# The pooling branch's mixing products taken by token half instead of by group

## The chip, the cores and the metric

The kernel runs on one core of one Trainium2 chip. The metric is device time in microseconds (us), the median of several runs. TensorE (PE) multiplies matrices, and its results can lie only in PSUM, which has eight banks of 128 partitions x 512 fp32 numbers. VectorE (DVE) and ScalarE (ACT) read PSUM, GpSimd (POOL) works in SBUF, and SyncE (SP) queues most of the transfers. Each engine takes its own instructions in the order in which they are written; semaphores hold one engine back for another.

## What is computed

One layer of a hybrid decoder on 1024 tokens of width 1024. The part that the change touches stands in the first block, where a pooling branch and an attention branch run side by side on the same input:

```python
h = rmsnorm(x, norm_mix_g)
u_pool, q, k, v, f_logit, g_logit = jnp.split(h @ w_in, IN_SPLITS, axis=-1)
# pooling: 4 groups of 128 channels, trailing-window mean minus the token
d = ...                                            # (tokens, 4 groups, 128)
y = jnp.einsum('bsgc,gcd->bsgd', d, pool_w)        # the mixing products
y_pool = (y.reshape(B, S, 512) * pool_scale) @ w_pool_out
y_fox = forgetting_attention(q, k, v, f_logit + b_forget) @ w_fox_out   # 8 heads of 64
x = x + (sigmoid(g_pool) * y_pool + sigmoid(g_fox) * y_fox) @ w_out
```

Cross-attention to 256 memory tokens, a SwiGLU feed-forward part and a last RMSNorm follow.

## The kernel before

**Units.** The attention runs as 32 units, u = 8 x (pair of heads) + i, where i is the block of 128 queries. In unit u PE computes the scores of u (L2562, called S here: 6 matmuls up to i = 3, 12 from i = 4), sometimes the products with the values of older units (L2530, V), and the transposes of unit u - 1 (L2539, T). DVE adds the forget bias and finds the largest score (L1915, two instructions), ACT takes the exponential (L1326) and DVE divides by the sum (L1927, L1929, called the norm of u here). The transposes in unit u + 1 wait for the norm of u. S of i < 4 writes banks 0 and 2, S of i >= 4 writes banks 0 to 3; T has banks 4 and 5, V has bank 6.

**Parts and fillers.** Other work of PE is put into the units as fillers, so that PE has something to do while DVE and ACT work on the scores. A unit has two parts, 2u and 2u + 1. For i >= 1 the order on PE is S(u), V, the first two groups of T (all of T, where i <= 4), part 2u, the rest of T, part 2u + 1; for i = 0 it is S, part 2u, V, first two groups of T, part 2u + 1, the rest of T. The tables `FIRST_FILL` (parts 0 to 23) and `NEXT_FILL` (parts 24 to 63) say how many fillers each part takes, in a fixed sequence of 88: 16 pieces of four products left over from the stage before, then 8 mixing products M0 to M7 (L2500, one group and one half of the tokens each), then 64 chunks of the products with `w_pool_out` (L2330 to L2332).

**The chunks.** The output of the pooling branch is made in 16 tiles, v = 0 to 15 (128 output channels c = v // 2, token half h = v % 2). Tile v takes four chunks, written v.0 to v.3 here, one for each group k, of three matmuls each. All 16 tiles are summed in PSUM bank 7. Chunk v.0 therefore waits until DVE has read tile v - 1 out of the bank: `pe.wait_ge(za_done, v)`. That read, `pool_gated(v)` (L1891, called za of v here), multiplies by the gate that SP has loaded into `g_st`. It needs chunk v.3, and its place among DVE's instructions is fixed by the part in which v.3 stands, through the table `GATED_IN`: for an even part it comes right behind the bias of u if i = 0 or i >= 4 and behind the norm of u if i is 1 to 3; for an odd part it comes behind the norm of u.

**The mixing products.** M m writes one bank of `MIX_BANK`; ACT takes the rounded high part `d_hi` (L1333, table `MIXED_IN`), DVE the rest `d_lo` (L1900, tables `LOWS_IN`, at the end of a unit, and `LOWS_LATE`, behind its bias). Before, m counts group by group (g = m // 2, h = m % 2), the banks 3, 7 and 1 go in turn, and tile 0 waits for all eight `d_lo`. Unit 12 is the first after unit 7 whose scores use banks 1 and 3, and its S waits for the first seven `d_lo`.

## Time and profile before

| what | value |
|---|---|
| median of 3 runs (1431.56 to 1432.39) | 1431.56 us |
| the profiled execution | 1431.69 us |
| its span, first to last instruction | 1429.6 us |
| PE busy | 1408.6 us, 99% |
| DVE busy | 992.0 us, 69% |
| ACT busy | 630.3 us, 44% |
| POOL busy | 551.4 us, 39% |
| mean granted TensorE clock | 0.998 |

The span and the 2.1 us around it make up the execution's own time. PE is busy nearly all the time, so the time is what PE has to do plus what it waits. Busy times of PE run over each other: a matmul of 128x512 is shown with some 0.39 us and the next one starts 0.23 us later. Costs are therefore read from one start to the next.

### The profile page before, as it was taken

What the parts mean: (1) busy time and instruction counts of PE and PEld (TensorE: products, weight loads), DVE (VectorE), ACT (ScalarE), POOL (GpSimd) and SP (SyncE); (2) the same over time, 40 slices, a digit from 0 to 9 for tenths busy, and PEclk for the clock granted to TensorE, in tenths of its full rate; (3) what the DMA queues carried; (4) which work ended last, traced back from release to release, by engine and by line L of the source; (5) the groups of instructions that cost most, each with busy time, mean ns of one, the idle gap of its engine ahead of it and who ended that gap; (6) DMA issues with size and microseconds to landing.
All of it is one profiled execution on the core that took longest, in us unless ns stands there. A gap on an engine that the chain in (4) does not pass through costs nothing.

```text
span 1429.6 us, 19604 instructions
## 1 busy us (share of the span) xinstructions
PE 1408.6 (99%) x7122; PEld 1154.2 (81%) x7122; DVE 992.0 (69%) x1442; ACT 630.3 (44%) x1196; POOL 551.4 (39%) x571
## 2 busy tenths in 40 slices
PE   8999999999999999999999999999999999999998
PEld 5878888887677788888888788888888888888886
DVE  7846495546866737877657877776776767785867
ACT  6545343335866644556444532233322332444445
POOL 5833243334545312013013654454444443354402
PEclk9999999999999999999999999999999999999999
DMA  8264264445332298214103112333332335883334
GB/s 215 50 130 117 56 136 101 74 82 202 116 97 84 65 294 215 80 60 133 60 0 147 66 58 93 110 111 111 110 110 84 109 111 204 303 283 100 89 104 148
DMA packets 107145, 172.14 MB, mean 120 GB/s; under 512 B 7293, under 2 KB 63121, under 8 KB 105514
## 3 DMA queue, kind: packets, MB, share of 16 engines
q1 hardware_dynamic: 98016, 146.59, 34.5%
q0 software_dynamic: 5408, 15.76, 4.3%
q10 hardware_dynamic: 3626, 8.54, 1.6%
q8 instruction: 58, 0.95, 0.3%
q14 instruction: 37, 0.30, 0.1%
HBM read 125.42 MB, written 42.30 MB: 117 GB/s over the span
## 4 chain that ended last, share of the span: by engine, by line
PE 88%; POOL 3%; ACT 2%; DMA 2%; DVE 2%; issue 1%; SPq 1%; DVEq 0%; ACTq 0%; POOLq 0%
PE ps L2330 27%; PE ps L2332 27%; PE ps L2331 27%; PE ps L2539 2%; PE ps L2530 2%; PE ps L2562 1%; POOL w_lo L873 1%; DMA w_raw<-in_w_xkv 1%; DMA e_raw<-in_w_in 1%; ACT prob L1326 1%; SPq L669 1%; PE ps L2392 1%; PE ps L2700 0%; ACT w_hi L1135 0%; POOL tok_f L922 0%
## 5 line engine op out<-in xcount | busy, mean ns | idle before, releaser
L2330 PE MATMUL ps<-t_lo,s_hi 128*128 128x512 f32 x308 | 119.9, 389 | 0.1
L2331 PE MATMUL ps<-t_hi,s_hi 128*128 128x512 f32 x308 | 119.8, 389 | 0.0
L2332 PE MATMUL ps<-t_hi,s_lo 128*128 128x512 f32 x308 | 119.8, 389 | 0.0
L2330 PE MATMUL ps<-h_lo_T,w_hi 128*128 128x512 f32 x256 | 100.5, 393 | 1.3 <-ACT u_t L1237 1.0
L1620 DVE TENSOR_TENSOR s_lo<-w_raw,s_hi 128x512 fp32r<-128x512 f32 x77 | 62.0, 805 | 56.3 <-ACT s_hi L1535 56.1
L1535 ACT ACTIVATE s_hi<-w_raw 128x512 fp32r<-128x512 f32 x77 | 48.7, 632 | 118.0 <-PE ps L2332 91.9
L2332 PE MATMUL ps<-h_hi_T,w_lo 128*128 128x512 f32 x256 | 99.7, 389 | 0.0
L2331 PE MATMUL ps<-h_hi_T,w_hi 128*128 128x512 f32 x256 | 99.6, 389 | 0.0
L1551 ACT ACTIVATE p_sb<-ps 128x512 f32<-128x512 f32 x22 | 13.1, 599 | 187.4 <-PE ps L2332 187.4
L2330 PE MATMUL ps<-hf_lo_T,w_hi 128*128 128x512 f32 x212 | 82.5, 389 | 0.0
L2331 PE MATMUL ps<-hf_hi_T,w_hi 128*128 128x512 f32 x212 | 82.5, 389 | 0.0
L2332 PE MATMUL ps<-hf_hi_T,w_lo 128*128 128x512 f32 x212 | 82.5, 389 | 0.0
L1620 DVE TENSOR_TENSOR w_lo<-s_sum,w_hi 128x512 fp32r<-128x512 f32 x64 | 49.3, 774 | 41.8 <-ACT w_hi L1186 41.5
L2330 PE MATMUL ps<-h_lo_B,w_hi 128*128 128x512 f32 x192 | 76.2, 397 | 0.9 <-DVE h_lo_B L1620 0.9
L1038 POOL TENSOR_TENSOR w_sum<-w_raw 128x512 f32<-128x512 f32 x11 | 14.2, 1292 | 158.7 <-DVE w_lo L1620 96.7
L2332 PE MATMUL ps<-h_hi_B,w_lo 128*128 128x512 f32 x192 | 74.9, 390 | 0.0
L2331 PE MATMUL ps<-h_hi_B,w_hi 128*128 128x512 f32 x192 | 74.8, 389 | 0.0
L2330 PEld LDWEIGHTS ps<-t_lo,s_hi 128*128 128x128 f32 x308 | 57.8, 188 | 12.6 <-issue 0.5
L2190 DVE TENSOR_TENSOR hq<-ps,p_sb 128x512 f32<-128x512 f32 x11 | 7.6, 690 | 86.9 <-DMA hs_dram<-h_sum 75.1
L2332 PEld LDWEIGHTS ps<-t_hi,s_lo 128*128 128x128 f32 x308 | 57.8, 188 | 12.0
L2331 PEld LDWEIGHTS ps<-t_hi,s_hi 128*128 128x128 f32 x308 | 57.8, 188 | 11.9
L862 POOL TENSOR_SCALAR ms<-ss 128x1 f32<-128x1 f32 x30 | 11.2, 374 | 141.6 <-ACT junk_x L1141 47.6
(402 smaller groups left out, 4319.0 us busy)
## 6 DMA issues: line engine op xcount, KB each, us to landing
w_raw<-hs_dram SPq DMA_DIRECT2D x77, 256.0 KB, 2.7
raw_p<-in_w_ffn_in SPq DMA_DIRECT2D x22, 512.0 KB, 4.5
w_raw<-in_w_ffn_in SPq DMA_DIRECT2D x22, 512.0 KB, 4.3
hs_dram<-h_sum SPq DMA_DIRECT2D x11, 1024.0 KB, 9.1
hs_dram<-hq SPq DMA_DIRECT2D x11, 768.0 KB, 7.1
wq_B<-in_w_ffn_out SPq DMA_DIRECT2D x8, 1024.0 KB, 7.8
raw_f<-in_w_in SPq DMA_DIRECT2D x14, 512.0 KB, 7.0
gate_dram<-c_st SPq DMA_DIRECT2D x28, 256.0 KB, 2.0
```

What stands on the lines that cost most here:

```text
L669: sp.dma_start(x_t[t][:], x2[tile_of(t), :]).then_inc(x_loaded[t], 16)
L873: nc.gpsimd.tensor_tensor(w_lo[n % SLOTS][:], w_raw[n % RAWS][:], w_hi[n % SLOTS][:].bitcast(FP32), ALU.subtract).then_inc(lo_ready, 1)
L1326: nc.scalar.activation(prob[u % 2][:, a, 0:n], prob[u % 2][:, a, 0:n], ACT.Exp, bias=neg_max[:, u % 2, a:a + 1], scale=-1.0, accum_out=pro ...
L1535: nc.scalar.activation(s2_hi[n % SLOTS2][:], s_raw(n % SLOTS2), ACT.Copy).then_inc(s_split_hi, 1)
L1620: nc.vector.tensor_tensor(out, a, hi.bitcast(FP32), ALU.subtract).then_inc(done, 1)
L2330: nc.tensor.matmul(dst, w_h, x_l, start=start, stop=False, skip_group_check=onto)
L2331: nc.tensor.matmul(dst, w_h, x_h, start=False, stop=False, skip_group_check=onto)
L2332: return nc.tensor.matmul(dst, w_l, x_h, start=False, stop=stop, skip_group_check=onto)
L2392: last = nc.tensor.matmul(ps[0:F_ROWS + HEADS, 5 * h, :], f_w[:, KD * h + 4 * part + j, :], (h_lo if x else h_hi)[ops[part]][:, j, :], sta ...
L2530: last = nc.tensor.matmul(ps[a * DH:(a + 1) * DH, 6, tile_of(v % 2)], v_sb[:, j, hc:hc + DH], turned(v, a)[:, tile_of(j)], start=j == 0, s ...
L2539: last = nc.tensor.transpose(ps[:, 4 + g % 2, tile_of(j - j0)], prob[v % 2][:, a, tile_of(j)], ident[:])
L2562: last = nc.tensor.matmul(ps[:, 2 * a + c // 4, 0:n * P], q[p % 2][head, tile_of(i)], k[p % 2][head, keys], start=term == 0, stop=term == 2)
```

## The change

The mixing products count half by half: h = m // 4, g = m % 4. With the first four `d_lo` (and the fifth, whose product uses bank 7) the even tiles of the first token half can be made, so tile 0 waits for five `d_lo` in place of eight and tile 1 for all eight. `MIX_BANK` becomes a list of eight, `MIX_FREED` says which `d_lo` each product waits for, and the tables for ACT and DVE are renumbered. S of unit 12 now waits for eight `d_lo`.

Tile 0 begins in part 21 (unit 10) in place of part 25 (unit 12). The two fill tables put one more M into part 17, one more into part 20, two chunks into part 21 and one each into parts 22 and 23; parts 29, 37, 41 and 57 each lose one chunk. No matmul, read or transfer is added or taken away.

```diff
-FIRST_FILL = (2, 2, 2, 2, 1, 0, 1, 1, 1, 0, 1, 0, 1, 0, 1, 1, 1, 1, 2, 1, 1, 1, 1, 0)
-NEXT_FILL = ((0, 2, 1, 1, 2, 2, 1, 2) + (1, 2, 1, 1, 2, 2, 2, 2, 2, 2, 1, 1, 1, 1, 1, 2)
-             + (1, 4, 2, 2, 2, 2, 2, 2, 2, 2, 1, 1, 1, 1, 1, 3))
+FIRST_FILL = (2, 2, 2, 2, 1, 0, 1, 1, 1, 0, 1, 0, 1, 0, 1, 1, 1, 2, 2, 1, 2, 2, 1, 1)
+NEXT_FILL = ((0, 2, 1, 1, 2, 1, 1, 2) + (1, 2, 1, 1, 2, 1, 2, 2, 2, 1, 1, 1, 1, 1, 1, 2)
+             + (1, 4, 2, 2, 2, 2, 2, 2, 2, 1, 1, 1, 1, 1, 1, 3))
 DEFER_DONE = {0: 0, 1: 1, 4: 2, 7: 3}
-MIXED_IN = {8: (0, 1), 9: (2, 3), 10: (4, 5, 6), 11: (7,)}
+MIXED_IN = {8: (0, 1, 2), 9: (3, 4, 5), 10: (6, 7)}
...
-GATED_IN = {part: v for part in range(24, 8 * T) for v in range(16) if FILL[part] <= 24 + 4 * v + 3 < FILL[part + 1]}
+GATED_IN = {part: v for part in range(20, 8 * T) for v in range(16) if FILL[part] <= 24 + 4 * v + 3 < FILL[part + 1]}
...
-LOWS_IN = {8: (0, 1), 9: (2, 3), 10: (4,), 11: (7,)}
-LOWS_LATE = {11: (5, 6)}
-MIX_BANK = (3, 7, 1)
+LOWS_IN = {8: (0, 1), 9: (3, 4), 10: (6,)}
+LOWS_LATE = {9: (2,), 10: (5,), 11: (7,)}
+MIX_BANK = (3, 7, 1, 3, 7, 1, 3, 1)
+MIX_FREED = {3: 1, 4: 2, 5: 3, 6: 4, 7: 6}
...
-                    g, h = divmod(m, 2)
+                    h, g = divmod(m, NG)
...
-                    elif m >= 3:
-                        pe.wait_ge(mix_lo, m - 2)
+                    elif m in MIX_FREED:
+                        pe.wait_ge(mix_lo, MIX_FREED[m])
...
                         if v == 0:
-                            pe.wait_ge(mix_lo, 2 * NG)
+                            pe.wait_ge(mix_lo, NG + 1)
                         else:
                             pe.wait_ge(za_done, v)
+                        if v == 1:
+                            pe.wait_ge(mix_lo, 2 * NG)
...
                     if u == 12:
-                        pe.wait_ge(mix_lo, 7)
+                        pe.wait_ge(mix_lo, 2 * NG)
```

Worked out from the tables, the last chunk of a tile and the first of the next (v.3 | v+1.0) stand in these parts:

| tiles | before | after |
|---|---|---|
| 0, 1 | 27, 28 | 23, 25 |
| 1, 2 | 29, 30 | 27, 28 |
| 2, 3 | 32, 33 | 30, 31 |
| 3, 4 | 35, 36 | 33, 33 |
| 4, 5 | 37, 38 | 36, 36 |
| 5, 6 | 39, 40 | 38, 39 |
| 6, 7 | 41, 42 | 40, 41 |
| 7, 8 | 45, 46 | 44, 45 |
| 8, 9 | 48, 49 | 47, 48 |
| 9, 10 | 49, 50 | 49, 49 |
| 10, 11 | 51, 52 | 51, 51 |
| 11, 12 | 53, 54 | 53, 53 |
| 12, 13 | 55, 56 | 55, 55 |
| 13, 14 | 57, 58 | 57, 58 |
| 14, 15 | 61, 62 | 61, 62 |

PE in units 10 to 12 of the kernel before: mixing products (out of `d_in_sb` and `pw_sb`), the scores of unit 11, its transposes, the last mixing product, the scores of unit 12.

```order
L2500 MATMUL ps<-d_in_sb,pw_sb 128x512 [waits mix_lo,d_in1,d_in0] x2
L2562 MATMUL ps<-k_hi1,q_lo1 128x512 [waits sc_biased,qk_lo]
L2562 MATMUL ps<-k_hi1,q_lo1 128x512
L2562 MATMUL ps<-k_hi1,q_hi1 128x512 x2
L2562 MATMUL ps<-k_lo1,q_hi1 128x512 x2
L2539 MATMUL ps<-ident,prob0 128x128 [waits pt_copied,prob_ready]
L2539 MATMUL ps<-ident,prob0 128x128 x2
L2539 MATMUL ps<-ident,prob0 128x128 [waits pt_copied]
L2539 MATMUL ps<-ident,prob0 128x128 x2
L2500 MATMUL ps<-d_in_sb,pw_sb 128x512 [waits mix_lo,d_in1,d_in0]
L2562 MATMUL ps<-k_hi1,q_lo1 128x512 [waits sc_biased,mix_lo,qk_lo]
```

The same place after: the last two mixing products, at once the two first chunks of tile 0 (`w_hi0` is the first piece of `w_pool_out`), then the scores of unit 11.

```order
L2501 MATMUL ps<-d_in_sb,pw_sb 128x512 [waits mix_lo,d_in1,d_in0] x2
L2331 MATMUL ps<-d_lo,w_hi0 128x512 [waits mix_lo,lo_ready]
L2332 MATMUL ps<-d_hi,w_hi0 128x512
L2333 MATMUL ps<-d_hi,w_lo0 128x512
L2331 MATMUL ps<-d_lo,w_hi0 128x512
L2332 MATMUL ps<-d_hi,w_hi0 128x512
L2333 MATMUL ps<-d_hi,w_lo0 128x512
L2565 MATMUL ps<-k_hi1,q_lo1 128x512 [waits sc_biased,qk_lo]
L2565 MATMUL ps<-k_hi1,q_lo1 128x512
L2565 MATMUL ps<-k_hi1,q_hi1 128x512 x2
L2565 MATMUL ps<-k_lo1,q_hi1 128x512 x2
L2542 MATMUL ps<-ident,prob0 128x128 [waits pt_copied,prob_ready]
```

The chunks moved ahead of the scores, and tile 0 waits for part of the `d_lo` alone.

PE in unit 16, part 33, before: the transposes of unit 15, then chunks 3.0 and 3.1, then the rest of the transposes.

```order
L2539 MATMUL ps<-ident,prob1 128x128 [waits pt_copied]
L2539 MATMUL ps<-ident,prob1 128x128 x3
L2330 MATMUL ps<-d_lo,w_hi0 128x512 [waits za_done,lo_ready]
L2331 MATMUL ps<-d_hi,w_hi0 128x512
L2332 MATMUL ps<-d_hi,w_lo0 128x512
L2330 MATMUL ps<-d_lo,w_hi0 128x512
L2331 MATMUL ps<-d_hi,w_hi0 128x512
L2332 MATMUL ps<-d_hi,w_lo0 128x512
L2539 MATMUL ps<-ident,prob1 128x128 [waits pt_copied]
L2539 MATMUL ps<-ident,prob1 128x128 x3
```

After: chunks 3.3 and 4.0 stand there. 4.0 uses the next piece of weights and waits for `za_done`.

```order
L2542 MATMUL ps<-ident,prob1 128x128 [waits pt_copied]
L2542 MATMUL ps<-ident,prob1 128x128 x3
L2331 MATMUL ps<-d_lo,w_hi0 128x512
L2332 MATMUL ps<-d_hi,w_hi0 128x512
L2333 MATMUL ps<-d_hi,w_lo0 128x512
L2331 MATMUL ps<-d_lo,w_hi1 128x512 [waits za_done,lo_ready]
L2332 MATMUL ps<-d_hi,w_hi1 128x512
L2333 MATMUL ps<-d_hi,w_lo1 128x512
L2542 MATMUL ps<-ident,prob1 128x128 [waits pt_copied]
L2542 MATMUL ps<-ident,prob1 128x128 x3
```

The end of a tile and the beginning of the next have moved from two parts into one, with nothing between them.

DVE in unit 16 before: two bias instructions, the read of bank 7 (za), the norm in four instructions, the bias of unit 17.

```order
L1915 ISA prob0,neg_max<-ps,negc1 128x128 [waits pt_done,negc_masked,sc_done]
L1915 ISA neg_max 128x1
L1915 ISA prob0,neg_max<-ps,negc2 128x128 [waits pt_done,negc_masked,sc_done]
L1915 ISA neg_max 128x1
L1891 TENSOR_TENSOR za1<-ps,g_st 128x512 [waits g_in0,po_done]
L1927 RECIPROCAL prob_inv<-prob_sum 128x1 [waits exp_ready]
L1929 TENSOR_SCALAR prob0<-prob0,prob_inv 128x128 [waits inv_ready]
L1927 RECIPROCAL prob_inv<-prob_sum 128x1 [waits exp_ready]
L1929 TENSOR_SCALAR prob0<-prob0,prob_inv 128x128 [waits inv_ready]
L1915 ISA prob1,neg_max<-ps,negc1 128x256 [waits negc_plain,pt_done,negc_masked,sc_done]
```

After: the read of bank 7 for tile 3 is written behind the norm.

```order
L1916 ISA prob0,neg_max<-ps,negc1 128x128 [waits pt_done,negc_masked,sc_done]
L1916 ISA neg_max 128x1
L1916 ISA prob0,neg_max<-ps,negc2 128x128 [waits pt_done,negc_masked,sc_done]
L1916 ISA neg_max 128x1
L1928 RECIPROCAL prob_inv<-prob_sum 128x1 [waits exp_ready]
L1930 TENSOR_SCALAR prob0<-prob0,prob_inv 128x128 [waits inv_ready]
L1928 RECIPROCAL prob_inv<-prob_sum 128x1 [waits exp_ready]
L1930 TENSOR_SCALAR prob0<-prob0,prob_inv 128x128 [waits inv_ready]
L1892 TENSOR_TENSOR za1<-ps,g_st 128x512 [waits g_in1,w_used]
L1916 ISA prob1,neg_max<-ps,negc1 128x256 [waits negc_plain,pt_done,negc_masked,sc_done]
```

The read that PE's next chunk waits for moved behind both reciprocals and both divisions of the unit.

## Rows read from the trace of the kernel before

**Rows 1.** Page, part 1: busy time, share of the span, instructions.

```profile
PE 1408.6 (99%) x7122; PEld 1154.2 (81%) x7122; DVE 992.0 (69%) x1442; ACT 630.3 (44%) x1196; POOL 551.4 (39%) x571
```

**Rows 2.** Waits of PE: who waited for whom, us in total, times, longest.

```profile
PE ps L2562 <- DVE d_lo L1900: 1.4, 1, 1.4
```

**Rows 3.** Busy by stretch: length, PE, PEld, DVE, ACT, POOL, clock, DMA share, GB/s.

```profile
410.00:501.00 91.00, 90.84 (x747) 71.65 (x745) 61.61 (x155) 58.55 (x143) 41.20 (x96) 1.00 0.24 79
```

**Rows 4.** Timeline of PE, units 11 and 12: start, us, instruction [idle before].

```profile
386.91 1.10 PE L2500 MATMUL ps<-d_in_sb,pw_sb 128*128 128x512 f32 x2
...
389.41 0.50 PE L2562 MATMUL ps<-k_hi,q_lo 64*128 64x512 f32 x2 [1.40 <-DVE d_lo L1900]
```

**Rows 5.** Timeline of DVE, same place.

```profile
387.90 1.41 DVE L1900 SCALAR_TENSOR_TENSOR d_lo<-ps,small,d_hi 128x512 fp32r<-128x512 f32 x2
```

**Rows 6.** Timeline of PE, unit 24: third and fourth chunk of a part.

```profile
461.45 0.39 PE L2330 MATMUL ps<-d_lo,w_hi 128*128 128x512 f32 x1
...
462.13 0.39 PE L2330 MATMUL ps<-d_lo,w_hi 128*128 128x512 f32 x1
...
462.59 0.40 PE L2332 MATMUL ps<-d_hi,w_lo 128*128 128x512 f32 x1
```

**Rows 7.** Timeline of DVE, unit 24: second division, then the read of bank 7.

```profile
462.44 0.29 DVE L1929 TENSOR_SCALAR prob<-prob,prob_inv 128x128 f32<-128x128 f32 x1
463.02 0.69 DVE L1891 TENSOR_TENSOR za<-ps,g_st 128x512 f32<-128x512 f32 x1 [0.29 <-PE ps L2332]
```

**Rows 8.** Timeline of PE, units 15 to 27: chunks at the places of the change.

```profile
410.36 0.47 PE L2330 MATMUL ps<-d_lo,w_hi 128*128 128x512 f32 x1
...
417.91 0.40 PE L2330 MATMUL ps<-d_lo,w_hi 128*128 128x512 f32 x1
...
426.06 0.40 PE L2330 MATMUL ps<-d_lo,w_hi 128*128 128x512 f32 x1
...
431.22 0.40 PE L2330 MATMUL ps<-d_lo,w_hi 128*128 128x512 f32 x1
...
437.43 0.40 PE L2330 MATMUL ps<-d_lo,w_hi 128*128 128x512 f32 x1
...
447.59 0.40 PE L2332 MATMUL ps<-d_hi,w_lo 128*128 128x512 f32 x1
...
448.40 0.48 PE L2330 MATMUL ps<-d_lo,w_hi 128*128 128x512 f32 x1
...
455.24 0.50 PE L2330 MATMUL ps<-d_lo,w_hi 128*128 128x512 f32 x1
...
473.02 0.39 PE L2330 MATMUL ps<-d_lo,w_hi 128*128 128x512 f32 x1
...
477.45 0.39 PE L2330 MATMUL ps<-d_lo,w_hi 128*128 128x512 f32 x1
```

**Rows 9.** Timeline of DVE, units 15 to 27: second bias (15), else second division.

```profile
409.42 1.22 DVE L1915 CUSTOM_DVE_ANT_0 prob<-ps,negc 128x1024 f32<-128x1024 f32 x1
...
419.07 0.29 DVE L1929 TENSOR_SCALAR prob<-prob,prob_inv 128x128 f32<-128x128 f32 x1
...
427.43 0.42 DVE L1929 TENSOR_SCALAR prob<-prob,prob_inv 128x384 f32<-128x384 f32 x1
...
432.21 0.62 DVE L1929 TENSOR_SCALAR prob<-prob,prob_inv 128x512 f32<-128x512 f32 x1
...
455.40 0.75 DVE L1929 TENSOR_SCALAR prob<-prob,prob_inv 128x1024 f32<-128x1024 f32 x1
...
473.00 0.42 DVE L1929 TENSOR_SCALAR prob<-prob,prob_inv 128x384 f32<-128x384 f32 x1
...
478.12 0.62 DVE L1929 TENSOR_SCALAR prob<-prob,prob_inv 128x512 f32<-128x512 f32 x1
```

**Rows 10.** Busy time by stretch, the first 5 us and near the end.

```profile
0.00:5.00 5.00, 2.32 (x3) 1.15 (x4) 0.81 (x4) 1.64 (x2) 1.22 (x10) 1.00 0.60 210
...
1424.00:1426.00 2.00, 0.00 (x0) 0.00 (x0) 0.87 (x2) 1.06 (x2) 0.81 (x2) 0.70 0.35 139
```

More of the change, by code:

```diff
@@ L1330, in _ @@
                 for m in MIXED_IN.get(u, ()):
-                    g, h = divmod(m, 2)
+                    h, g = divmod(m, NG)
                     act.wait_ge(mix_done, m + 1)
-                    nc.scalar.activation(d_hi[:, g, half_of(h)], ps[:, MIX_BANK[m % 3], :], ACT.Copy,
+                    nc.scalar.activation(d_hi[:, g, half_of(h)], ps[:, MIX_BANK[m], :], ACT.Copy,
                                          scale=ps_scale[:, g:g + 1]).then_inc(mix_hi, 1)
@@ L1897, in mixed_lo @@
             def mixed_lo(m):
-                g, h = divmod(m, 2)
+                h, g = divmod(m, NG)
                 dve.wait_ge(mix_hi, m + 1)
-                nc.vector.scalar_tensor_tensor(out=d_lo[:, g, half_of(h)], in0=ps[:, MIX_BANK[m % 3], :],
+                nc.vector.scalar_tensor_tensor(out=d_lo[:, g, half_of(h)], in0=ps[:, MIX_BANK[m], :],
                                                scalar=ps_scale[:, g:g + 1], in1=d_hi[:, g, half_of(h)].bitcast(FP32),
@@ L2492, in fill @@
                     m = f - 16
-                    g, h = divmod(m, 2)
+                    h, g = divmod(m, NG)
                     pe.wait_ge(d_in[0], 48)
@@ L2497, in fill @@
                         pe.wait_ge(def_ev, 4)
-                    elif m >= 3:
-                        pe.wait_ge(mix_lo, m - 2)
-                    nc.tensor.matmul(ps[:, MIX_BANK[m % 3], :], pw_sb[:, g, :], d_in_sb[:, g, half_of(h)],
+                    elif m in MIX_FREED:
+                        pe.wait_ge(mix_lo, MIX_FREED[m])
+                    nc.tensor.matmul(ps[:, MIX_BANK[m], :], pw_sb[:, g, :], d_in_sb[:, g, half_of(h)],
                                      start=True, stop=True).then_inc(mix_done, 1)
```

## The prediction

> **What bounds the kernel now.** I began with the busy shares: PE is busy for 1408.6 of 1429.6 us [rows 1], so the time is PE's work and whatever PE waits for. The waits of PE show where there is something to win in this stage: the largest one here is 1.4 us, the scores of unit 12 waiting for a `d_lo` [rows 2]. The busy time by stretch says how much else there is: from 410 to 501 us, where units 16 to 31 and most of the chunks run, PE is busy for 90.84 of 91.00 us [rows 3], that is, PE waits 0.16 us in all. The fillers cover the attention chain completely there. A chunk moved in that stretch wins nothing by itself, and every wait that is added there goes straight into the time.
>
> **What the change removes: the wait of unit 12.** Before, the last mixing product starts at 386.91 and, after it, PE stands idle for 1.40 us until the scores of unit 12 begin at 389.41 [rows 4]. DVE takes two `d_lo` from 387.90 to 389.31 meanwhile [rows 5], and the seventh of them frees the bank. After the change the eighth `d_lo` is awaited, but the products come one to two units sooner, and four chunks and the transposes of unit 11's turn stand between the last product and those scores. A chunk takes 0.68 us (461.45 to 462.13 [rows 6]), four take 2.7 us; the last `d_lo` is written right behind the bias of unit 11, so it should come in time. The 1.40 us go.
>
> Two small costs stand against them. M7 needs bank 1, so it waits for the sixth `d_lo`, which is written behind the bias of unit 10: between nothing and one `d_lo` (1.41 / 2 = 0.7 us [rows 5]); I take 0.2, since the chunk order puts the bias about where PE arrives. And pairs of chunks are broken up or stand behind transposes, for which I take 0.1. The four chunks added before part 24 and the four taken out of parts 29, 37, 41 and 57 are the same work, 4 x 0.68 us on either side: no gain and no loss. What is won at this end is 1.4 - 0.3 = 1.1 us. The parts that lose a chunk lose 0.68 us of cover; the norm awaited next had been done about as long before, so I add nothing there.
>
> **What the change adds: PE and DVE hand bank 7 over with nothing in between.** Everything sums in one bank. Before, the last chunk of a tile and the first of the next always stood in different parts, with scores or transposes between them, or with so much DVE time that the read was over. In the new tables six of these pairs stand in one part (3|4, 4|5 and 9|10 to 12|13), and five more have moved closer (2|3 and 5|6 to 8|9). Chunk v+1.0 waits for `za_done`, and behind it on PE stand the rest of the transposes and the scores of the next unit, thus also the bias, the exponential and the norm: all of it moves by the whole wait.
>
> The least such a handover costs: the last matmul of tile 9 starts at 462.59 and ends at 462.99, DVE's read starts at 463.02 and takes 0.69 [rows 6, 7], to 463.71. PE takes up work 0.10 after DVE's end (387.90 + 1.41 = 389.31, start 389.41 [rows 4, 5]), so at 463.81, where the next chunk would have started at 462.59 + 0.23 = 462.82. That is **0.99 us**, with DVE free. Where the read is written behind the norm of the unit, DVE reaches it only at the end of the second division, and the chunk starts 0.69 + 0.10 = 0.79 us after that end. I compare this with the time at which the chunk would start without a wait, by the row of the chunk that stands in its place now.
>
> Tile 2|3, unit 15: the read follows the second bias, which ends at 409.42 + 1.22 = 410.64 [rows 9]. The chunk could start at 411.43 and wants to at 410.36 [rows 8]: 1.07. Tile 3|4, unit 16, behind the norm: 419.07 + 0.29 + 0.79 = 420.15 against 417.91: 2.24. Tile 4|5, unit 18: 427.43 + 0.42 + 0.79 = 428.64 against 426.06: 2.58. Tile 5|6, unit 19, two parts with no transposes between: 432.21 + 0.62 + 0.79 = 433.62 against 431.22: 2.40. Tile 6|7, unit 20, read ahead of the norm, DVE waiting for PE: 0.99 (the fourth chunk wants 437.43 [rows 8], and DVE's bias is long over). Tile 7|8, unit 22, six transposes between: the last matmul 447.59 + 0.40, then 0.03 + 0.69 + 0.10, is 448.81 against 448.40: 0.41. Tile 8|9, units 23 and 24, only the short scores between: 455.40 + 0.75 + 0.79 = 456.94 against 455.24: 1.70. Tile 9|10, unit 24: 462.44 + 0.29 + 0.79 = 463.52 [rows 7] against 462.13 [rows 6]: 1.39. Tile 10|11, unit 25, norm early: 0.99. Tile 11|12, unit 26: 473.00 + 0.42 + 0.79 = 474.21 against 473.02: 1.19. Tile 12|13, unit 27: 478.12 + 0.62 + 0.79 = 479.53 against 477.45: 2.08, but this norm is late now because a read and an `o_lo` stand ahead of its bias, and the read will be over sooner, so I take 1.8. [rows 8, 9] hold all of these where no other group is named. Tiles 0|1, 1|2, 13|14 and 14|15 have parts and work between them as before and cost nothing.
>
> All times are relative to the scores of their unit, and since bias, exponential and norm hang on PE's scores and transposes, they move with them. The sum is 1.07 + 2.24 + 2.58 + 2.40 + 0.99 + 0.41 + 1.70 + 1.39 + 0.99 + 1.19 + 1.8 = **16.8 us**.
>
> The strict order on DVE is what makes 2.24 out of 0.99 in unit 16. The Trainium skill says the same under PSUM — Partial Sum Buffer, Engine vs sequencer instructions: the queues of ScalarE, VectorE and GpSimdE are strict first in, first out. If DVE could take the read ahead of the waiting norm, the sum would be that of the first rival below. No row here shows a read overtaking a norm.
>
> **Other queues.** Where the read is written ahead of the norm (tiles 2, 6, 7), DVE now waits there for PE with the norm queued behind it. In unit 20 this pushes the norm about to the moment when its transposes want it: 0 to 0.3 us, kept for the range. SP loads the gate of tile v + 2 once tile v is read; reads of the same half are still more than one tile apart, so the gates should be there. POOL's masks hang on the biases and move along. ACT loses the wait for M7 and gains nothing else.
>
> **The sum.** 1431.69 (the profiled execution: span 1429.6 and 2.1 around it) + 16.8 - 1.1 = 1447.4. The median lies 0.13 below that execution, so 1447.3; the small overlap of neighbouring DVE instructions, which I have counted as if they stood end to end, makes me take **1447.1 us**, 1.1% slower.
>
> **Rivals.** First, the norms are not what ends the waits: DVE is free each time PE finishes a tile, be it that the norms come sooner once PE has stood still, be it that I have misplaced a read. Then ten handovers cost 0.99 and one 0.41: 10.3 - 1.1 = +9.2, or 1440.8 us. For it: a wait of PE gives ACT and DVE time to catch up. Against it: the norm hangs on scores and transposes that PE issues in the same unit, so it cannot get ahead of them. 9%.
>
> Second, the clock. In the two microseconds from 1424, without a matmul, the granted clock averages 0.70, thus it has gone from 2.4 to 1.2 GHz part of the way through [rows 10]; in the first five microseconds PE is busy for only 2.32 and the clock stays at 1.00. Four of the new waits are about 2 to 2.6 us long. If each of them took the clock to the lower level for one unit's worth of work, say 6 us at half speed, it would cost 3 us each, 12 in all: 1459 us. The Trainium skill, in TensorE: Matmul & The Clock Gate, What's actually happening, holds that the throttled state is the default and activity releases it, which is the mechanism of this rival; the trace agrees as far as the end of the kernel goes. Against it: PE stood for 1.40 us before unit 12 and the granted clock reads 1.00 in the stretch that follows [rows 3], and there is work on both sides of every wait. 5%.
>
> Third, **not slower**: the count that a chunk waits for is met when PE gets there, because the reads are issued sooner than I place them, or the order on PE keeps enough between. It decides from the point where the read ends before the chunk's turn, 0.99 us after the tile's last matmul at the least. All waits would be zero and only the 1.1 us of the front remain: 1430.5 us. For it: before, 15 handovers cost 0.16 us together at most [rows 3]. Against it: in the new order nothing at all stands between 3.3 and 4.0, and one bank cannot be read and summed into at once. 4%. A gain of over 0.2% would need more waits than PE has in the stage: 1%.
>
> **How the numbers follow.** The forecast has 77%, with a spread of some 3 us either way from the eleven terms; the three rivals have 9, 5 and 4%, and the rest is a mixture. The range 1441.5 to 1451 holds the forecast and what lies between it and the first rival. About 0.2%, or 2.9 us, is what a measurement of this kernel can tell from no change: faster 1%, same 5%, slower 94%.
>
> **What would show it.** In the profile after, the 1.4 us wait on `d_lo` is gone, and a wait of PE's chunk on DVE's `za` stands first: about 11 times, some 15 to 17 us, the longest near 2.6 in unit 18. Busy PE from 410 to about 515 falls to some 85%. The time up to unit 15 is 1.1 us or so ahead once its four extra chunks are counted. Wrong would be: chunk 4.0 starting within 1 us of 3.3's end (the first rival), a granted clock under 1.00 in the stage (the second), or no wait on `za` (the third).

## The result

The kernel after takes **1448.83 us** (median of 4 runs, 1448.19 to 1448.95) against 1431.97 us for the kernel before (4 runs, 1431.56 to 1432.99). The ratio is 1.0119, with a 95% interval of 1.0107 to 1.0131: 16.9 us slower. The profiled execution has a span of 1446.8 us and took 1448.95 us. The prediction was 1447.1 us, in a range of 1441.5 to 1451.

Busy time by engine of the kernel after, as in [rows 1]. PE has the same 7122 instructions. It is shown busy 4.7 us longer and the span has grown by 17.2 us, so most of what was added is PE standing still.

```profile
PE 1413.3 (98%) x7122; PEld 1154.8 (80%) x7122; DVE 993.9 (69%) x1442; ACT 629.8 (44%) x1196; POOL 553.1 (38%) x571
```

The waits of PE, as in [rows 2] (who waited for whom, us in total, times, longest). The wait on `d_lo` is gone from the list. The first line is new: a chunk that waits for the read of bank 7, 11 times.

```profile
PE ps L2331 <- DVE za L1892: 14.4, 11, 2.4
...
PE ps L2542 <- DVE prob L1930: 1.0, 3, 0.5
```

The stretch with the chunks, as in [rows 3] (length, PE, PEld, DVE, ACT, POOL, clock, DMA share, GB/s). PE is busy for 90.57 of 105.00 us, 86%, where before it was 90.84 of 91.00. The granted clock is 0.98.

```profile
410.00:515.00 105.00, 90.57 (x728) 69.02 (x727) 59.89 (x150) 56.20 (x139) 40.52 (x96) 0.98 0.21 68
```

The 11 waits on the timeline of PE, units 15 to 19. The number in brackets is PE's idle time ahead of the instruction.

```profile
412.51 0.47 PE L2331 MATMUL ps<-d_lo,w_hi 128*128 128x512 f32 x1 [0.79 <-DVE za L1892]
...
422.25 0.47 PE L2331 MATMUL ps<-d_lo,w_hi 128*128 128x512 f32 x1 [2.02 <-DVE za L1892]
...
434.43 0.47 PE L2331 MATMUL ps<-d_lo,w_hi 128*128 128x512 f32 x1 [2.37 <-DVE za L1892]
...
441.46 0.47 PE L2331 MATMUL ps<-d_lo,w_hi 128*128 128x512 f32 x1 [2.32 <-DVE za L1892]
```

Units 20 to 24.

```profile
448.81 0.47 PE L2331 MATMUL ps<-d_lo,w_hi 128*128 128x512 f32 x1 [0.87 <-DVE za L1892]
...
459.65 0.47 PE L2331 MATMUL ps<-d_lo,w_hi 128*128 128x512 f32 x1 [0.22 <-DVE za L1892]
...
467.75 0.47 PE L2331 MATMUL ps<-d_lo,w_hi 128*128 128x512 f32 x1 [1.34 <-DVE za L1892]
```

Units 24 to 27.

```profile
475.70 0.47 PE L2331 MATMUL ps<-d_lo,w_hi 128*128 128x512 f32 x1 [0.94 <-DVE za L1892]
...
481.53 0.47 PE L2331 MATMUL ps<-d_lo,w_hi 128*128 128x512 f32 x1 [0.88 <-DVE za L1892]
...
488.95 0.47 PE L2331 MATMUL ps<-d_lo,w_hi 128*128 128x512 f32 x1 [0.98 <-DVE za L1892]
...
495.29 0.47 PE L2331 MATMUL ps<-d_lo,w_hi 128*128 128x512 f32 x1 [1.63 <-DVE za L1892]
```

These are exactly the eleven handovers that the prediction named, from 2|3 to 12|13. DVE in unit 18 shows what the long ones wait for: division, division, and only then the read, from 433.60 to 434.28. PE starts 0.15 us later.

```profile
433.06 0.16 DVE L1928 RECIPROCAL prob_inv<-prob_sum 128x1 f32<-128x1 f32 x1
433.26 0.42 DVE L1930 TENSOR_SCALAR prob<-prob,prob_inv 128x384 f32<-128x384 f32 x1
433.60 0.68 DVE L1892 TENSOR_TENSOR za<-ps,g_st 128x512 f32<-128x512 f32 x1
```

And the granted clock (the third number from the end) in two stretches behind the wait of 2.02 us in unit 16. It was 1.00 everywhere else from 408 to 516 us. 0.50 is the lower of the two levels, 1.2 GHz.

```profile
422.00:424.00 2.00, 1.75 (x7) 1.45 (x8) 0.10 (x1) 0.00 (x0) 0.00 (x0) 0.65 0.33 109
424.00:426.00 2.00, 2.00 (x12) 1.58 (x11) 0.00 (x0) 1.19 (x2) 0.00 (x0) 0.50 0.06 23
```

### The profile page after: what moved, and what is told of

It reads as the page before. It is cut to its first block, busy times and chain, and to the rows that moved or that the text cites. A ratio compares the mean times of both kernels' runs of the same rounds, so it can differ in the third digit from the quotient of the medians.

```text
span 1446.8 us, 19604 instructions
## 1 busy us (share of the span) xinstructions
PE 1413.3 (98%) x7122; PEld 1154.8 (80%) x7122; DVE 993.9 (69%) x1442; ACT 629.8 (44%) x1196; POOL 553.1 (38%) x571
## 4 chain that ended last, share of the span: by engine, by line
PE 87%; ACT 3%; DVE 3%; POOL 3%; issue 2%; DMA 2%; DVEq 0%; ACTq 0%; POOLq 0%
PE ps L2331 27%; PE ps L2333 26%; PE ps L2332 26%; PE ps L2533 2%; PE ps L2542 2%; PE ps L2565 1%; ACT prob L1327 1%; DMA w_raw<-in_w_xkv 1%; ACT prob_t L1318 1%; POOL w_lo L874 1%; PE ps L2393 1%; PE ps L2703 0%; DVE prob L1930 0%; PE ps L2501 0%; DVE za L1892 0%
```

## The experiments

All kernels are the kernel after with one edit, unless it is said otherwise. Each was compared with the kernel before on the same chip; the median of before was 1431.83, 1431.65 and 1431.81 us in the three groups of runs. The last number of `NEXT_FILL` belongs to part 63.

### The order of the mixing products alone

The fill tables of before, in the numbering of the mixing products of after:

```diff
-FIRST_FILL = (..., 1, 1, 1, 2, 2, 1, 2, 2, 1, 1)
+FIRST_FILL = (..., 1, 1, 1, 2, 2, 1, 2, 0, 0, 0)
-NEXT_FILL = ((0, 2, 1, 1, 2, 1, 1, 2) + (1, 2, 1, 1, 2, 1, 2, 2, 2, 1, 1, 1, 1, 1, 1, 2)
-             + (1, 4, 2, 2, 2, 2, 2, 2, 2, 1, 1, 1, 1, 1, 1, 3))
+NEXT_FILL = ((0, 2, 1, 1, 2, 2, 1, 2) + (1, 2, 1, 1, 2, 2, 2, 2, 2, 2, 1, 1, 1, 1, 1, 2)
+             + (1, 4, 2, 2, 2, 2, 2, 2, 2, 2, 1, 1, 1, 1, 1, 3))
```

> The mixing products go by token half as in the changed kernel, but no chunk moves: tile 0 begins in part 25 again and the fill table from part 24 on is that of before. Theory (the tile edges on bank 7 cost the time, the chunks ahead of unit 12 win the 1.1 us): no wait on za, and nothing won either, since with no chunks between the last mixing product and the scores of unit 12 the eighth d_lo, written behind the bias of unit 11, is late again (a wait of 1.2 to 1.7 us on d_lo): 1431 to 1433 us. Rival (the new order of the mixing products or their waits cost part of the time): above 1434 us. Rival (the order alone wins the wait): near 1430.7 us and no wait on d_lo.

Measured: 1431.79 us, ratio 0.9999 (0.999 to 1.0008). There is no wait on the read of bank 7, and the wait of the scores of unit 12 on `d_lo` is back with 1.36 us, at 390.18. The time is in the range that the expectation gave. The order of the products is harmless and, without chunks to put ahead of unit 12, worth nothing.

### The early tile with whole tiles kept apart

The mixing products and the front (the four chunks ahead of unit 12) are as in after. The four chunks that must go for them are taken out of parts 57, 58, 59 and 63:

```diff
-NEXT_FILL = ((0, 2, 1, 1, 2, 1, 1, 2) + (1, 2, 1, 1, 2, 1, 2, 2, 2, 1, 1, 1, 1, 1, 1, 2)
-             + (1, 4, 2, 2, 2, 2, 2, 2, 2, 1, 1, 1, 1, 1, 1, 3))
+NEXT_FILL = ((0, 2, 1, 1, 2, 2, 1, 2) + (1, 2, 1, 1, 2, 2, 2, 2, 2, 2, 1, 1, 1, 1, 1, 2)
+             + (1, 4, 2, 2, 2, 2, 2, 2, 2, 1, 0, 0, 1, 1, 1, 2))
```

> The changed kernel up to part 24 with its four early chunks, but from part 25 on the fill table of before, so that every tile stands where the one before it stood and no tile edge lies inside a part; the four chunks are taken out at the end (parts 57, 58, 59 and 63 lose one each). Theory: no wait of PE on za above 0.1 us, the 1.4 us wait of unit 12 gone, perhaps 0.3 to 0.8 us of waits near units 29 to 31 where cover is missing: 1430.4 to 1431.5 us, against 1432.0 before. Rival (the early chunks themselves, or the missing cover, cost the time): 1440 us or more.

Measured: 1431.69 us, ratio 0.9999 (0.999 to 1.0008), span 1429.4. That is 17.1 us less than the kernel after, with everything else of the change in place. One wait on the read is left, 0.16 us, and one new wait of the transposes on `prob_t`, 0.58 us at 488.07, where a part has lost its only chunk. The time is 0.2 us above the expected range, so the gain of the front does not show in it. But **the whole loss comes from where the tables put the chunks**, and none from the mixing products or from tile 0 in unit 10.

### One handover in the kernel before

The converse: the kernel *before*, one chunk moved from part 36 to part 35, so that 3.3 and 4.0 stand side by side in unit 17.

```diff
-... (1, 2, 1, 1, 2, 2, 2, 2, 2, 2, 1, 1, 1, 1, 1, 2)
+... (1, 2, 1, 2, 1, 2, 2, 2, 2, 2, 1, 1, 1, 1, 1, 2)
```

> The kernel before, with one chunk moved from part 36 to part 35: the last chunk of tile 3 and the first of tile 4 stand side by side in unit 17, with nothing between them. Nothing else is changed, in particular not the mixing products. Theory (the adjacency alone costs, by the place of the read): in the trace of before, the read of tile 3 ends at 422.67 + 0.68 = 423.35, so the chunk starts at 423.45 where it could start at 422.04: +1.4 us, 1433.2 to 1433.6 us, with one wait of PE on za of 1.2 to 1.4 us. First rival (PE has slack for one such wait): 1431.8 to 1432.2 us. Second rival (the waits of the kernel after come from the new order of the mixing products and not from adjacency): no wait on za here, 1431.8 us.

Measured: 1433.17 us, ratio 1.0009 (1.0000 to 1.0018), so +1.5 us. The interval begins at no change, so the trace is the better evidence. PE, then DVE, at that place:

```profile
421.48 0.40 PE L2332 MATMUL ps<-d_hi,w_lo 128*128 128x512 f32 x1
423.27 0.47 PE L2330 MATMUL ps<-d_lo,w_hi 128*128 128x512 f32 x1 [1.39 <-DVE za L1891]
```

```profile
422.17 0.35 DVE L1929 TENSOR_SCALAR prob<-prob,prob_inv 128x256 f32<-128x256 f32 x1
422.44 0.68 DVE L1891 TENSOR_TENSOR za<-ps,g_st 128x512 f32<-128x512 f32 x1
```

The read stands behind the norm, from 422.44 to 423.12, and the chunk starts at 423.27. The same handover, 3|4, waits here in the kernel before, in unit 17 in place of 16 and for 1.39 us in place of 2.02, with nothing of the change to the mixing products. The 1.39 us are idle time as the profile shows it, counted from the end of a matmul that would have overlapped the next one by 0.16 us, so a wait costs some 0.2 us more than its bracket. By start, the scores of unit 19 come 1.41 us later than before, in an execution that was 0.23 us ahead up to unit 16: 1.6 us.

### Other banks for five tiles

Tiles 4, 10 and 12 go to bank 1, tiles 5 and 11 to bank 3, the others stay in bank 7. The scores of units 20 and 28, the next ones that write banks 1 and 3, wait for the reads of these tiles. `OUT_FREED` says which read has freed the bank of tile v; the matmuls and the read take the bank out of `OUT_BANK`.

```diff
+OUT_BANK = {4: 1, 5: 3, 10: 1, 11: 3, 12: 1}
...
-pe.wait_ge(za_done, v)
+pe.wait_ge(za_done, OUT_FREED[v])
...
+                    if u in (20, 28):
+                        pe.wait_ge(za_done, {20: 6, 28: 13}[u])
```

> The changed kernel, order and fill unchanged, but tiles 4, 10 and 12 sum in bank 1 and tiles 5 and 11 in bank 3, which no scores use in units 16 to 19 and 24 to 27; scores of units 20 and 28 wait for the reads of those tiles. Theory (bank 7 is what PE and DVE hand over): the waits at tile edges 3|4, 4|5, 5|6, 9|10, 10|11, 11|12 and 12|13 go, 11.1 us of shown idle, 1.2 us of start-to-start distance and 1.3 us at the lower clock; waits on za of about 3.2 us stay: 1434.5 to 1436.5 us. Rival (the waits are for DVE's or ACT's time and come back at the next transposes): 1443 us or more.

Measured: 1436.22 us, ratio 1.0030 (1.0018 to 1.0042). The order of chunks is that of after, and 12.6 us are back. The waits of PE:

```profile
PE ps L2333 <- DVE za L1894: 3.2, 4, 1.3
...
PE ps L2569 <- issue: 1.6, 2, 0.8
```

The four that are left on `za` are 2|3, 6|7, 7|8 and 8|9, which still share a bank; the two of 0.80 and 0.79 us marked "issue" are the scores of units 20 and 28, which carry the new waits. So it is the one bank, and not the nearness of the chunks as such, that costs.

### The read ahead of the norm, everywhere

Every read of bank 7 is written right behind the bias of its unit, for both parts.

```diff
-                if 2 * u in GATED_IN and (i >= 4 or i == 0):
-                    pool_gated(GATED_IN[2 * u])
+                for part in (2 * u, 2 * u + 1):
+                    if part in GATED_IN:
+                        pool_gated(GATED_IN[part])
...
-                if 2 * u in GATED_IN and 0 < i < 4:
-                    pool_gated(GATED_IN[2 * u])
-                if 2 * u + 1 in GATED_IN:
-                    pool_gated(GATED_IN[2 * u + 1])
```

> The changed kernel with one thing other: DVE's read of bank 7 always stands right behind the bias of its unit, ahead of the norm. Theory: where the read stood behind the norm (units 16, 18, 19, 23, 24, 26, 27) the wait falls to what a handover costs with DVE free, 0.8 to 0.9 us shown as idle, and unit 16 no longer has a wait long enough for the clock to fall; waits on za 7 to 9 us in all in place of 14.4: 1440 to 1443 us. Rival (the place of the read does not matter, PE waits for its own order): 1448 to 1449 us.

Measured: 1452.12 us, ratio 1.0145 (1.0131 to 1.0159): 3.3 us *slower* than the kernel after, where a gain of 6 to 9 was expected. **The expectation was wrong**, though its first half came true. The waits of PE:

```profile
PE ps L2328 <- DVE za L1892: 8.0, 10, 0.9
PE ps L2539 <- DVE prob L1931: 7.2, 7, 2.7
```

The waits on the read fell from 14.4 to 8.0 us, none of them above 0.9, and are as short as was expected. But the transposes now wait 7.2 us for the norm (1.0 in after), and two single waits of 1.49 and 1.38 us came up before the scores of units 12 and 24, whose `d_lo` and `k_lo` stand behind a read on DVE. Where v.3 comes late in its unit, DVE stands at the read with the norm queued behind it; at the reads DVE waited 34.9 us for PE, in 15 waits, against 3.6 in 2 waits in after. The worst of them, in unit 29, on DVE, POOL and PE:

```profile
497.98 0.69 DVE L1892 TENSOR_TENSOR za<-ps,g_st 128x512 f32<-128x512 f32 x1 [2.78 <-PE ps L2330]
...
499.24 0.16 DVE L1929 RECIPROCAL prob_inv<-prob_sum 128x1 f32<-128x1 f32 x1
499.44 2.44 DVE L1931 TENSOR_SCALAR prob<-prob,prob_inv 128x640 f32<-128x640 f32 x1
```

```profile
499.19 2.34 POOL L874 TENSOR_TENSOR w_lo<-w_raw,w_hi 128x1024 fp32r<-128x1024 f32 x1 [3.64 <-ACT w_hi L1136]
```

```profile
501.93 0.76 PE L2539 MATMUL ps<-ident,prob 128*128 128x128 f32 x5 [2.75 <-DVE prob L1931]
```

Here something else joins in. The second division takes 2.44 us, where the same shape took 0.55 us in the kernel after (502.20), and it runs beside POOL's `w_lo` of 2.34 us that began at 499.19. In unit 18 a division of 128x384 took 2.62 us in place of 0.42, beside POOL's `w_lo` of 2.36 us, and in unit 31 one of 128x1024 took 2.65 in place of 0.75 (521.22), beside a `w_lo` of 2.50. The waits for the norm behind these three are 2.75, 1.24 and 1.41 us, 5.4 of the 7.2. An estimate from these rows: had the three divisions kept their usual length, 0.9 of the 5.4 us would be left. So most of the new waiting for the norm is owed to the slow divisions, and the norm held up behind the read was the smaller part: those 0.9 us and a fourth wait of 0.79 (515.00).

This is more than one coincidence. In the 13 traces of this case 23 divisions of the norm began while a `w_lo` of this size ran on POOL (one of them 0.03 us ahead of it), and none ended before that `w_lo`. In the kernel before there are two, of 1.67 us (375.88) and 0.82 us (461.52) where 0.29 is usual. Two that began more than 0.4 us ahead of the `w_lo` kept their length. No edit moved POOL's work by itself.

The four executions took 1451.51 to 1454.69 us, with a mean granted clock of 0.997 or 0.998 in the two shortest and 0.995 in the longest, so part of the median is the clock. The profiled one, 1451.51 us, has one fall of the clock, as after has, and is 2.6 us slower than after's.

### The read ahead of the norm, where the last chunk comes early

The same edit for parts 33, 38, 49, 51, 53 and 55 alone (tiles 3, 5, 9, 10, 11, 12):

```diff
-                if 2 * u in GATED_IN and (i >= 4 or i == 0):
-                    pool_gated(GATED_IN[2 * u])
+                for part in (2 * u, 2 * u + 1):
+                    if part in GATED_IN and (part in (33, 38, 49, 51, 53, 55) or part % 2 == 0 and (i >= 4 or i == 0)):
+                        pool_gated(GATED_IN[part])
...
-                if 2 * u in GATED_IN and 0 < i < 4:
+                if 2 * u in GATED_IN and 0 < i < 4 and 2 * u != 38:
                     pool_gated(GATED_IN[2 * u])
-                if 2 * u + 1 in GATED_IN:
+                if 2 * u + 1 in GATED_IN and 2 * u + 1 not in (33, 49, 51, 53, 55):
                     pool_gated(GATED_IN[2 * u + 1])
```

> The kernel after; the reads of bank 7 for the six tiles whose last chunk stands in parts 33, 38, 49, 51, 53 and 55 are written right behind the bias of their unit, ahead of the norm. The others stay where they are. These are parts of units with i = 0, 1, 2 and 3 in which the last chunk comes soon behind the scores, so DVE should get there in time for the norm. Theory (the strict order on DVE makes the waits longer than the 0.99 us of a bare handover; reading first helps where the last chunk comes early in the unit and hurts where it comes late, as in unit 29 of the run with all reads first): six waits shrink to 0.8 to 0.9 each, some 4.5 us less, the clock stays at 1.00 in unit 16 (1.3 us less), and up to 1 us comes back as waits for the norm: 1443.0 to 1445.0 us. Rival (whatever read stands ahead of the norm sends the wait on to the norm, by as much as it saves): 1448 to 1452 us, with new waits of the transposes for DVE's division in units 16, 19, 24 to 27.

Measured: 1444.58 us, ratio 1.0089 (1.0075 to 1.0103): 4.3 us less than after. The six waits are 0.87 to 0.88 us each, and no new wait of the transposes has come up. PE in unit 16, then DVE:

```profile
419.37 0.40 PE L2334 MATMUL ps<-d_hi,w_lo 128*128 128x512 f32 x1
420.64 0.47 PE L2332 MATMUL ps<-d_lo,w_hi 128*128 128x512 f32 x1 [0.88 <-DVE za L1892]
```

```profile
419.80 0.69 DVE L1892 TENSOR_TENSOR za<-ps,g_st 128x512 f32<-128x512 f32 x1 [3.61 <-PE ps L2334]
420.41 0.15 DVE L1929 RECIPROCAL prob_inv<-prob_sum 128x1 f32<-128x1 f32 x1
420.60 0.29 DVE L1931 TENSOR_SCALAR prob<-prob,prob_inv 128x128 f32<-128x128 f32 x1
...
```

The read now starts 0.43 us after the start of the tile's last matmul, and the chunk follows at 420.64: 1.27 us from start to start where 0.23 is usual. The wait that was 2.02 us is 0.88. So the surplus over the bare handover came from the norm that stood ahead of the read, as the prediction had it for those tiles.

### Where the clock falls

First, one edge taken out: 4.0 is moved from part 33 to part 34.

```diff
-... (1, 2, 1, 1, 2, 1, 2, 2, 2, 1, 1, 1, 1, 1, 1, 2)
+... (1, 1, 2, 1, 2, 1, 2, 2, 2, 1, 1, 1, 1, 1, 1, 2)
```

> The kernel after, with one chunk moved from part 33 to part 34, so that between the last chunk of tile 3 (part 33) and the first of tile 4 (part 34) the rest of the transposes and the scores of unit 17 stand. Nothing else is changed. Theory (each wait costs what its own read of bank 7 costs; the fall of the granted clock to 1.2 GHz in unit 16 belongs to the 2.02 us wait): the wait of 2.02 + 0.17 us goes and, with it, the 1.2 to 1.3 us of work at half speed; the chunk moved may leave a wait of up to 0.6 behind. 1448.8 - 2.2 - 1.3 + (0 to 0.6) = 1445.3 to 1445.9 us; the granted clock reads 1.00 from 410 to 515 us. First rival (the clock falls at some other of the two waits above 2.3 us once the first is gone): 1446.4 to 1447.2 us, with a low clock in unit 18 or 19. Second rival (the wait comes back at another place, since DVE and PE only stand still elsewhere): 1448.8 us.

Measured: 1446.49 us, ratio 1.0102 (1.0087 to 1.0118). The main theory asked for 1445.3 to 1445.9; the time is that of its **first rival**. The wait in unit 16 is gone, and the granted clock is 1.00 there. It falls at the end of the next one instead, 2.36 us long, in unit 18:

```profile
430.00:432.00 2.00, 1.52 (x4) 1.26 (x5) 0.34 (x1) 0.03 (x1) 1.89 (x1) 0.58 0.25 84
432.00:434.00 2.00, 2.00 (x8) 1.21 (x8) 0.00 (x0) 0.00 (x0) 1.84 (x5) 0.57 0.29 76
```

Then the kernel after once more, unchanged:

> The kernel after, unchanged, profiled a second time, for the place of the low clock. If one certain wait brings the fall of the granted clock, it is seen in unit 16 again, from 422 to 426 us, and nowhere else. If it depends on something that differs from run to run, it falls at another of the waits, or not at all. The time is 1448.2 to 1449.0 us in the first case; in the second it may differ by up to 1.7 us, which is what the longest stretch at a low clock has cost so far.

Measured: 1450.21 us (one execution), span 1448.1. The eleven waits are the same to within 0.02 us, save 9|10 with 0.88 in place of 0.94 (14.3 us in all), and the clock fell twice: in unit 16, as before, and again in unit 20, behind the wait of 2.34 us.

```profile
422.00:424.00 2.00, 1.84 (x6) 1.47 (x7) 0.02 (x1) 0.00 (x0) 0.00 (x0) 0.59 0.38 127
424.00:426.00 2.00, 2.00 (x13) 1.55 (x11) 0.00 (x0) 1.20 (x2) 0.00 (x0) 0.56 0.01 4
442.00:444.00 2.00, 2.00 (x9) 1.32 (x9) 0.00 (x0) 0.00 (x0) 0.00 (x0) 0.71 0.43 131
444.00:446.00 2.00, 2.00 (x18) 1.77 (x16) 0.79 (x3) 0.00 (x0) 0.00 (x0) 0.50 0.00 0
446.00:448.00 2.00, 2.00 (x25) 1.83 (x22) 0.79 (x4) 0.86 (x3) 1.36 (x5) 0.94 0.00 0
```

The second fall cost 1.5 us: by the start of unit 21's scores this execution is 1.45 us behind the first one, which up to unit 20 it had matched within 0.14. So the fall is not tied to a certain wait of the program. The run with some reads first shows a third case. It passed a wait of 2.36 us in unit 18 with the clock at 1.00, and the clock fell in unit 24 behind one of 1.36 us. The products with the values, in that run and in the kernel after:

```profile
463.21 0.47 PE L2332 MATMUL ps<-d_lo,w_hi 128*128 128x512 f32 x1 [1.36 <-DVE za L1892]
...
464.08 2.70 PE L2534 MATMUL ps<-odd_t,v_sb 128*64 128x128 f32 x24
466.56 2.25 PE L2534 MATMUL ps<-prob_t,v_sb 128*64 128x128 f32 x28
```

```profile
468.61 1.53 PE L2533 MATMUL ps<-odd_t,v_sb 128*64 128x128 f32 x24
469.97 1.70 PE L2533 MATMUL ps<-prob_t,v_sb 128*64 128x128 f32 x28
```

They take 4.66 us (464.08 to 468.74, the start of the transposes) in place of 2.99 (468.61 to 471.60): 1.7 us lost. In the runs with no wait on `za` above 1.4 us (the mixing order alone, whole tiles apart, other banks, one handover) the clock did not fall from 408 to 516 us. The Trainium skill, in TensorE: Matmul & The Clock Gate, What's actually happening, holds that the clock follows PE's recent activity. These runs agree in so far as only the kernels with many waits show a fall; what decides between a wait of 1.36 us that brings it and one of 2.36 that does not, they leave open.

### Is there a version that beats both?

Three placements of the four chunks to be taken out, all with the front of after and the two ends of every handover in different parts, as before. Their last 16 numbers of `NEXT_FILL` (the rest of it is that of before):

```diff
-+ (1, 4, 2, 2, 2, 2, 2, 2, 2, 1, 1, 1, 1, 1, 1, 3))
++ (1, 4, 2, 2, 2, 2, 2, 2, 1, 1, 1, 0, 1, 1, 1, 2))
++ (1, 4, 2, 2, 2, 2, 1, 1, 1, 1, 1, 1, 1, 1, 1, 3))
++ (1, 4, 1, 1, 1, 1, 2, 2, 2, 2, 1, 1, 1, 1, 1, 3))
```

> The mixing products by token half and tile 0 in unit 10, as in the kernel after, with every last and next first chunk in different parts, as in the kernel before, up to tile 13; tile 14 is summed up to part 60, so that part 58 has a chunk (the run with whole tiles kept apart had none there and showed a wait of 0.58 us). Theory: the 1.4 us wait for the d_lo before unit 12 is gone, nothing new waits in units 12 to 31, and the 0.58 us wait is gone: 1430.8 to 1431.6 us, 0.2 to 1.0 below the kernel before. Rival (the chunks that stand ahead of unit 12 only move the same waiting to the first units, as the run with whole tiles kept apart gave 1431.7): 1431.6 to 1432.2 us, no difference from before.

> The kernel after (mixing products by token half, tile 0 in unit 10), but the four chunks that the front has taken over are taken out of parts 54 to 57 (units 27 and 28), one each, and the other parts are as in the kernel before. Every last and next first chunk then stand in different parts. Theory (what is won in front of unit 12 stays won if the parts that lose a chunk have time left over): in the trace of before, the norm of unit 27 is done at 478.74 and its transposes start at 480.65, 1.9 us later, and two chunks are 1.4 us, so nothing is lost: 1.2 us less than before, 1430.4 to 1430.8 us, with S of unit 31 some 1.0 to 1.2 us ahead of before by the same start. Rival (the gain is lost again whichever parts are cut): 1431.4 to 1432.0 us, with a wait of transposes for DVE's division, or of a chunk for za, in units 27 to 29.

> As the run with parts 54 to 57 cut, but the four chunks are taken out of parts 50 to 53 (units 25 and 26), one each. Theory: in the trace of before, the norm of unit 25 is done 3.5 us before its transposes, that of unit 26 at 473.42, 1.3 us before its transposes at 474.69; two chunks are 1.4 us, so up to 0.1 us is lost: 1430.5 to 1430.9 us. Rival (the gain is lost again): 1431.4 to 1432.0 us, with waits in units 25 to 28.

| cut in | us | ratio, interval |
|---|---|---|
| parts 56, 57, 59, 63 | 1431.18 | 0.9996 (0.9987 to 1.0005) |
| parts 54 to 57 | 1431.53 | 0.9998 (0.9989 to 1.0007) |
| parts 50 to 53 | 1430.93 | 0.9994 (0.9985 to 1.0003) |

All three are 17 to 18 us faster than the kernel after. None can be told from before by its time: each interval holds no change. The first lies in its expected range, the second 0.7 us above it, the third 0.03 above it. The traces tell more. With parts 50 to 53 cut, the scores of unit 31 start here, beside those of before:

```profile
494.00 0.50 PE L2565 MATMUL ps<-k_hi,q_lo 64*128 64x512 f32 x2
```

```profile
494.86 0.50 PE L2562 MATMUL ps<-k_hi,q_lo 64*128 64x512 f32 x2
```

That is 0.86 us ahead, where at 337 us, ahead of the mixing products, the two traces are level within 0.03. With parts 54 to 57 cut, two waits take 0.65 us back: the scores of unit 28 wait for a `neg_max`, and the transposes in unit 29 wait 0.50 us for the norm.

```profile
479.24 0.50 PE L2565 MATMUL ps<-k_hi,q_lo 64*128 64x512 f32 x2 [0.15 <-DVE neg_max L1916]
...
485.90 0.76 PE L2542 MATMUL ps<-ident,prob 128*128 128x128 f32 x5 [0.50 <-DVE prob L1930]
```

The expectation of that run (1430.4 to 1430.8) missed: unit 27 had 1.9 us to spare by the trace of before, but the units behind it had not. This execution was also the latest of the 13 traces at 337 us, where no edit has touched anything yet: the scores there start between 336.56 and 337.51, 0.67 us after those of before in this one. Such differences are why one trace's span is not compared below 1 us here, but positions relative to that point are. With parts 56, 57, 59 and 63 cut, the same wait of 0.50 us stands in unit 29 (486.76), and 14|15 waits 0.16 us. By the traces the gain of the front is real, about 1 us, and one placement of three kept most of it, the one that takes the chunks where nothing is short. The times do not show it clear of the noise.

## Why the prediction was right

**The place.** It said that PE has no slack from 410 to 501 us and that each wait goes into the time. The run with one handover in the kernel before shows this for a single one: 1.39 us of wait, 1.5 us of time.

**The front.** Predicted: 1.1 us won. Compared by the start of unit 12's scores, after stands at

```profile
391.21 0.50 PE L2565 MATMUL ps<-k_hi,q_lo 64*128 64x512 f32 x2
```

which is 1.80 us later than before, with four chunks more (4 x 0.68 = 2.7). The two traces were already 0.27 us apart at 337 us, before any of this, so the front won 2.7 - 1.5 = 1.2 us. From the scores of unit 0 to those of unit 12 after takes 54.10 us, and before 52.57. The eight other traces with this front, and with the reads placed there as in after, take 54.08 to 54.14. The wait of M7, which the prediction took at 0.2, is 0.09 us (385.74).

**The waits, term by term.** Measured is how much further after falls behind before, from one unit's scores to the next, with 0.68 us added back where a part has lost a chunk. The row of 3|4 covers units 16 and 17, over which the low clock reaches.

| tiles | predicted | measured | shown as idle |
|---|---|---|---|
| 2, 3 | 1.07 | 1.03 | 0.79 |
| 3, 4 | 2.24 | 3.68 | 2.02 |
| 4, 5 | 2.58 | 2.60 | 2.37 |
| 5, 6 | 2.40 | 2.58 | 2.32 |
| 6, 7 | 0.99 | 1.12 | 0.87 |
| 7, 8 | 0.41 | 0.47 | 0.22 |
| 8, 9 and 9, 10 | 3.09 | 2.42 | 1.34 + 0.94 |
| 10, 11 | 0.99 | 1.12 | 0.88 |
| 11, 12 | 1.19 | 1.25 | 0.98 |
| 12, 13 | 1.8 | 1.91 | 1.63 |
| sum | 16.8 | 18.2 | 14.4 |

Eight of eleven terms hold within 0.2 us. One was too small: 3|4 has the low clock in it. Its wait of 2.02 us and the 0.2 that a bracket leaves out are the 2.24 predicted, and the other 1.4 us are the clock. Without them 16.7 us are left for the waits.

Two were too large by 0.3 us each, 8|9 and 9|10, both in unit 24. Chunk 9.0 starts 1.89 us after the scores of unit 24 in place of 0.48, so 8|9 cost 1.4 and not 1.70; chunk 10.0 starts at 475.70 in place of 474.38 + 0.23, so 9|10 cost 1.1 and not 1.39. In both the norm comes sooner, counted from PE's work in the unit, than in the rows of before by which the prediction placed it. For 8|9, a read of bank 7 (450.86) stood ahead of the bias of unit 23 before, and after it does not: that bias starts 1.69 us behind the unit's scores in place of 2.19. For 9|10, the first division of unit 24 had been a slow one in the kernel before, beside POOL's `w_lo`; the prediction took the second division's 462.44 as given.

```profile
459.85 2.40 POOL L873 TENSOR_TENSOR w_lo<-w_raw,w_hi 128x1024 fp32r<-128x1024 f32 x1
```

```profile
461.52 0.82 DVE L1929 TENSOR_SCALAR prob<-prob,prob_inv 128x128 f32<-128x128 f32 x1
```

In the kernel after that `w_lo` (470.56 to 472.93) is over before the norm begins:

```profile
473.99 0.58 DVE L1930 TENSOR_SCALAR prob<-prob,prob_inv 128x128 f32<-128x128 f32 x1
...
474.87 0.68 DVE L1892 TENSOR_TENSOR za<-ps,g_st 128x512 f32<-128x512 f32 x1
```

The division of 0.58 us runs beside a shorter POOL operation (474.02 to 474.48). The read starts 0.1 us after the end of 9.3 (474.38 + 0.39), so the norm hardly held it: 0.94 us of idle time is nearly the bare handover. That ACT and DVE catch up while PE stands still, as the first rival had it, is not what the rows show: the norm's first instruction comes 5.18 us after the products with the values begin, and 5.19 before (473.79 - 468.61, 461.32 - 456.13).

The bare handovers (6|7, 10|11) are some 0.1 us larger than predicted: after a wait, a chunk's first matmul takes 0.31 us to the next start in place of 0.23 (434.43 to 434.74). That the sum of the waits comes out within 0.1 us of the prediction's 16.8 is therefore in part luck: two terms are 0.6 us too large together, and the others make up for it.

**The sum.** 16.7 of waits and 1.4 of clock, less 1.2 won at the front, make 16.9, and the medians differ by 16.9. The prediction added 15.7, less 0.2 for DVE instructions that overlap. Its 1447.1 is 1.7 us too low: 1.4 are the low clock, which the sum held at nothing and the second rival alone had, and the median of before itself came out 0.4 higher with a fourth run (1431.97).

**The rivals.** The first (bare handovers, 1440.8) is out: only at 9|10 did the norm no longer hold the read, and for another reason than the one it gave. The run with some reads first shows for 3|4, 5|6 and 12|13 that the norm was what made them longer: their idle time falls from 2.02, 2.32 and 1.63 us to 0.87 or 0.88. For 4|5 and 8|9 it is read from the timelines. The Trainium skill's rule under PSUM — Partial Sum Buffer, Engine vs sequencer instructions, that DVE takes its queue strictly in order, was borne out twice: a read written behind the norm ran behind it, and a norm written behind a waiting read waited with it (unit 29 of the run with all reads first: the read had waited 2.78 us, the first reciprocal followed it at 498.58). The second (the clock) came in part: I had priced four falls at 3 us each, and the traces show one or two of 1.4 to 1.7 us. The argument against it, that 1.40 us of waiting before unit 12 had left the clock at 1.00, did not carry: in another run the clock fell behind a wait of 1.36 us, with longer waits in the units ahead of it. The third (not slower) is what the placements with whole tiles apart do, and not the change as made.

**What would show it.** The `d_lo` wait was gone, the wait on `za` stood first, 11 times, the longest in unit 18, busy PE was 86%. Its sum was said to be 15 to 17 us and is shown as 14.4, because idle time in the list begins at the end of a matmul and not where the next would have started.
